# A transformer-like stack in one launch: the mixer's block sums move ahead of three steps of a gemm, and a copy on VectorE moves ahead of a subtraction

## The reference

```python
u = rmsnorm(h, norm_mix[l])
proj = u @ w_in[l]
u_ssm, q, k, v = jnp.split(proj, [D_SSM, D_SSM + D_ATTN, D_SSM + 2 * D_ATTN], axis=-1)
y_ssm = s5_branch(u_ssm, ...)              # x_t = Abar x_{t-1} + Bbar u_t, y_t = Re(C x_t) + D u_t
y_attn = stick_breaking_attention(q, k, v) # A[t,s] = beta[t,s] * prod_{s<j<t} (1 - beta[t,j])
```

## Time and profile before

| | |
|---|---|
| median of three runs | 1427.44 us (1426.12 to 1428.05) |
| the profiled execution | 1426.22 us |
| its span (first to last instruction) | 1424.4 us |
| TensorE busy | 1387.7 us, 97% of the span |
| VectorE busy | 962.6 us, 68% |
| ScalarE busy | 736.3 us, 52% |
| granted TensorE clock, mean | 0.995 |
| the four steps of the mixer | about 44 to 226 us of the span |

### The profile page before, as it was taken

One profiled execution on the slowest core, in us unless ns is written; L12 is line 12 of the kernel. 1 busy time (PEld: TensorE's weight loads), 2 busy tenths in 40 slices (PEclk: granted clock), 3 DMA queues, 4 the chain that ended last, 5 costly groups with the idle time before them and its releaser, 6 DMA issues.

```text
span 1424.4 us, 18408 instructions
## 1 busy us (share of the span) xinstructions
PE 1387.7 (97%) x6984; PEld 1163.5 (82%) x6984; DVE 962.6 (68%) x1343; ACT 736.3 (52%) x1038; POOL 70.8 (5%) x81
## 2 busy tenths in 40 slices
PE   7999999999999999999999999999999999999997
PEld 4888888788888888888877999878878888887876
DVE  7989984424654445444469777554879999998574
ACT  6777776222432223222246444333558888888452
POOL 2000000000200000000020000002100000000311
PEclk9999999999999999999999999999999999999998
DMA  6111102222222232322221211222221121211311
GB/s 222 43 60 60 60 27 92 89 95 107 94 89 89 99 109 89 103 86 106 89 89 60 89 59 59 104 89 89 89 89 60 61 86 59 85 63 44 119 60 59
DMA packets 19241, 118.22 MB, mean 83 GB/s; under 512 B 2400, under 2 KB 3680, under 8 KB 5616
## 3 DMA queue, kind: packets, MB, share of 16 engines
q1 hardware_dynamic: 18896, 116.38, 22.9%
q0 software_dynamic: 288, 1.05, 0.2%
HBM read 115.32 MB, written 2.10 MB: 82 GB/s over the span
## 4 chain that ended last, share of the span: by engine, by line
PE 75%; DVE 8%; ACT 3%; issue 2%; POOL 0%; DVEq 0%; POOLq 0%; ACTq 0%
PE ps L520 23%; PE ps L522 23%; PE ps L521 22%; PE ps L1015 1%; DVE wlo L1832 1%; PE ps L1048 1%; PE ps L1005 1%; PE ps L1046 1%; DVE st L2314 1%; PE ps L1007 1%; DVE stlo L2317 1%; ACT sthi L1193 1%; POOL pp L503 0%; ACT whi L1193 0%; PE ps L616 0%
## 5 line engine op out<-in xcount | busy, mean ns | idle before, releaser
L520 PE MATMUL ps<-uhi,whi 128*128 128x512 f32 x1100 | 436.3, 397 | 7.8 <-DVE ulo L2351 3.7
L522 PE MATMUL ps<-uhi,wlo 128*128 128x512 f32 x1100 | 429.7, 391 | 0.0
L521 PE MATMUL ps<-ulo,whi 128*128 128x512 f32 x1100 | 428.9, 390 | 0.0
L1832 DVE TENSOR_TENSOR wlo<-wraw,whi 128x2048 fp32r<-128x2048 f32 x104 | 241.0, 2320 | 98.7 <-ACT whi L1193 97.2
L1193 ACT ACTIVATE whi<-wraw 128x2048 fp32r<-128x2048 f32 x105 | 200.3, 1908 | 162.4 <-PE ps L522 160.5
L520 PEld LDWEIGHTS ps<-uhi,whi 128*128 128x128 f32 x1100 | 207.0, 188 | 55.5 <-issue 6.4
L522 PEld LDWEIGHTS ps<-uhi,wlo 128*128 128x128 f32 x1100 | 206.7, 188 | 44.6
L521 PEld LDWEIGHTS ps<-ulo,whi 128*128 128x128 f32 x1100 | 207.2, 188 | 40.0
L520 PE MATMUL ps<-hdhi,whi 128*128 128x512 f32 x256 | 99.6, 389 | 0.0
L521 PE MATMUL ps<-hdlo,whi 128*128 128x512 f32 x256 | 99.6, 389 | 0.0
L522 PE MATMUL ps<-hdhi,wlo 128*128 128x512 f32 x256 | 99.6, 389 | 0.0
(11 more groups left out here) (444 smaller groups left out, 2460.9 us busy)
## 6 DMA issues: line engine op xcount, KB each, us to landing
wraw<-wstream SPq DMA_DIRECT2D x105, 1024.0 KB, 4.8
h<-xT SPq DMA_DIRECT2D x4, 512.0 KB, 5.5
outT<-h SPq DMA_DIRECT2D x8, 256.0 KB, 2.9
s5b<-s5p_d SPq DMA_DIRECT2D x1, 1024.0 KB, 12.2
pe_in<-pT POOLq DMA_DIRECT2D x2, 512.0 KB, 3.8
cst_in<-cst_d SPq DMA_DIRECT2D x5, 64.0 KB, 10.1
reset<-cst_d SPq DMA_DIRECT2D x1, 256.0 KB, 11.2
ones<-cst_d SPq DMA_DIRECT2D x1, 64.0 KB, 2.5
```

The lines of the kernel that those rows point to most:

```text
L520: nc.tensor.matmul(out, lh, rh, start=start, stop=False, skip_group_check=True)
L521: nc.tensor.matmul(out, lh, rl_, start=False, stop=False, skip_group_check=True)
L522: mm = nc.tensor.matmul(out, ll, rh, start=False, stop=stop, skip_group_check=True)
L1832: V.tensor_tensor(wlo[:, slot, :], wraw[:, slot, :], whi[:, slot, :], ALU.subtract).then_inc(lo_done, 1)
```

## The change

On TensorE, the gemm of the next q is cut in two: five of its eight steps stay in their place, then the block sums and the triangle follow, and the other three steps come behind the triangle, ahead of the kernels. On VectorE, the copy that repeats the input maps leaves `turn_in` and becomes a function of its own, `repeat_maps`, called between `softplus(0)` and `fail_lo(0)`; since it overwrites Es, which the block sums read, it now carries the wait for them.

```diff
@@ -742,9 +742,10 @@
                 scores(0)
                 u_blocks(i)
                 pe.wait_ge(v_ready, i + 1)
-                gemm(n, 0, one(0), 256, uhi, ulo)
+                gemm(n, 0, one(0), 256, uhi, ulo, part=range(5))
                 block_sums()
                 log_weights(0)
+                gemm(n, 0, one(0), 256, uhi, ulo, part=range(5, DC))
                 kernels()
                 scores(1)
@@ -2063,16 +2064,20 @@
+                def repeat_maps():
+
+                    dve.wait_ge(f_done, 2 * i + 1)
+                    dve.wait_ge(in_gen, i + 1)
+                    V.tensor_copy(Es[:, :, :].rearrange("p r (q j c) -> p (r q) j c", q=QP, j=L),
+                                  ET[:, :, :, 0:1, :].rearrange("p r q j c -> p (r q) j c").to_broadcast([P, 2 * QP, L, 32])
+                                  ).then_inc(rep_ready, 1)
+
                 def turn_in():
                     f = ps[:, S0:S0 + 2, :].rearrange("p r (q n) -> p r q n", q=QP)
                     dve.wait_ge(f_done, 2 * i + 1)
                     dve.wait_ge(table_ready, i + 1)
                     own.do(V.tensor_tensor(rin[:, :, :, :], f, cos2, ALU.mult))
                     V.tensor_tensor(zst[:, :, :, :], f, sin2, ALU.mult).then_inc(f_used, 1)
-                    dve.wait_ge(in_gen, i + 1)
-                    V.tensor_copy(Es[:, :, :].rearrange("p r (q j c) -> p (r q) j c", q=QP, j=L),
-                                  ET[:, :, :, 0:1, :].rearrange("p r q j c -> p (r q) j c").to_broadcast([P, 2 * QP, L, 32])
-                                  ).then_inc(rep_ready, 1)
@@ -2119,6 +2124,7 @@
                 out_maps(i)
                 softplus(0)
+                repeat_maps()
                 fail_lo(0)
                 turn_in()
                 w_lo(0)
```

## The result

| | before | after |
|---|---|---|
| median | 1427.73 us (11 runs, 1426.12 to 1428.83) | 1430.77 us (11 runs, 1429.50 to 1432.80) |
| profiled execution | 1426.22 us | 1430.61 us |
| its span | 1424.4 us | 1428.8 us |
| first scores of step 0 to second scores of step 3 | 45.20 to 197.06: 151.86 us | 45.32 to 200.58: 155.26 us |

The ratio of after to before is 1.0024, 95% interval 1.0016 to 1.0032: the change makes the kernel slower, by 3.4 us with an interval of 2.3 to 4.6 (the two medians are 3.04 us apart). The forecast was 1.8 us, which I called no change; the median lies just inside the range given, 1427.3 to 1431.0.

What follows compares the result with a forecast made beforehand. The prediction took TensorE to bound the mixer, hardly waiting there. Step costs 0.49 + 0.41 + 0.41 + 0.49 = 1.80 us, put on the median of 1427.44, gave 1429.2 us, range 1427.3 to 1431.0.

Steps and rivals of the forecast that it cites:

- What bounds the mixer: In the mixer's four steps TensorE hardly waits, so each microsecond lost in a step's head reaches the program's end.
- The new wait for athi: Between block sums and triangle TensorE would newly wait 1.45 us in steps 1 to 3; step 0's wait becomes 2.46.
- The copy on VectorE: Between softplus and low half the copy into Es fits in idle time, 0.45 us ahead of 100.20, and costs nothing.
- The kernels' wait goes, and they take 1.70: Behind the three late gemm steps the kernels no longer wait (1.06 us before) and take 1.70 us.
- 0.49 per step, 0.41 where VectorE's chain has room: Second scores come 0.49 us later per step; steps 1 and 2 pass on 0.41, steps 0 and 3 all 0.49.
- The clock: Rival: step 0's 2.46 us wait makes TensorE's clock fall, costing 1.7 us more, 1430.9 us in all; 7 in 100.
- the two rivals at 1430.8 and 1430.9: VectorE's low half pushed back, 1430.8 us, 5 in 100; one clock fall in step 0, 1430.9 us, 7 in 100.
- The rival of the pushed low half: Late block sums delay VectorE's copy, so atlo slips 0.4 us and a step costs 0.9: 1430.8 us; 5 in 100.

Runs made afterwards that it cites:

- e4: The change in steps 1 to 3 alone, step 0 ordered as before: mixer 153.33 us (before 151.86), time ratio to before 1.0004.
- e3: The change plus eight matmuls with unread results in step 0's wait for athi: mixer 153.85 us (with the change 155.26), time ratio to before 1.0013.
- e1: The kernel before with TensorE's gemm cut 5 + 3 alone, VectorE's copy in its old place: mixer 155.30 us, time ratio to before 1.0026.
- e8: The change in step 0 alone, steps 1 to 3 ordered as before: mixer 153.80 us, time ratio to before 1.0013.
- e2: The kernel before with VectorE's copy into Es moved alone, the gemm whole: mixer 155.04 us, time ratio to before 1.0038.
- e5: The change with the gemm cut 6 + 2 instead of 5 + 3: mixer 153.17 us, time ratio to before 0.9999.
- e6: The kernel before with the gemm cut 7 + 1, the copy into Es in its old place: mixer 151.78 us, time ratio to before 1.0004.
- e9: The kernel before with the copy into Es made by GpSimd instead of VectorE: mixer 151.75 us (before 151.86), time ratio to before 0.9998.
- e10: As e9, and half of VectorE's scan moved ahead of the first weights' low part: mixer 149.52 us, time ratio to before 0.9992.
- e7: The kernel before with second scores ahead of the kernels on TensorE, ScalarE and VectorE reordered to match: mixer 154.65 us, time ratio to before 1.0026.

## Why the prediction was wrong, point by point

- **What bounds the mixer: right.** TensorE waits hardly anywhere, and what it loses in the head of a step stays lost. e4 and e3 show about 0.5 us per step arriving at the end of the stretch.
- **The new wait for athi: right in kind and size.** I computed 1.45 us in steps 1 to 3 from start to start, and got 102.29 - (99.17 + 1.70) = 1.42; in step 0 2.46, and got 2.45. The view of waits counts less (1.18 and 2.18, 5.8 in all where I had written 6.5 to 7), as it counts from the modelled end of the last matmul.
- **The copy on VectorE: right.** It fits into the idle time, 0.42 us ahead of athi where I had said 0.45; e1 shows that it also buys nothing.
- **The kernels' wait goes, and they take 1.70: right.** 109.09 - 107.39 = 1.70.
- **0.49 per step, 0.41 where VectorE's chain has room: right to 0.1.** Measured 0.54, 0.52 and 0.52 in steps 1 to 3, with 0.06 to 0.07 given back between steps. Without the clock the sum is 3.40 - 1.44 = 1.96 us, and 1.99 in e3, where 1.80 stood in the sum.
- **The clock: this is the step that failed.** The sum put the clock at nothing. I wrote the mechanism down with its place, one fall in step 0, and its price, "1.8 + 1.7 = 3.5, so 1430.9", but gave it 7 in 100. The fall came in all three profiles of this order in step 0 (after, e1, e8), and cost 1.44 us where 1.7 was written. My grounds were that a wait of 1.36 us in step 0 had left the clock at 1.00. A wait 1.8 times as long is outside of what such a row can vouch for. The trace of before has nearer rows, which the prediction did not read: TensorE waits 2.11 us for ulo until 936.33, and the granted clock stays at 1.00; it waits 2.43 us for rstd until 1416.45, and the granted clock is 0.57 from 1416 to 1422, though only one matmul runs there. One of two is no ground for 7 in 100. The rule cited from the Trainium skill, "TensorE: Matmul & The Clock Gate", section "Loop structure matters more than you think", pointed the right way; the trace agrees with it here, with 0.50 granted after a wait of 2.18 us, and does not in other places (last section).
- **The chances.** With the forecast's sum of 1.8 so near to the 2.85 us that bound no change, a term of 1.4 to 1.7 us decided between no change and slower. The case that carried it had to be settled before the other digits. That the median, 1430.77, lies inside the range says nothing for the forecast's own sum: the range reached up to the two rivals at 1430.8 and 1430.9.
- **The rival of the pushed low half** did not occur in the change; e2 shows it, with 0.86 us of wait for atlo in step 1.

## What to carry to other kernels

A wait that ends a chain on another engine is not shortened by giving the waiting engine its work in another order: before work is moved out of a place, ask what runs beneath it, here the 6.8 us from ScalarE's first function of the scores (93.39) to athi (100.17), and compare its length with the work that remains. Where a move leaves TensorE standing in one piece, look through the whole trace for waits of that length, read the granted clock behind each, and give a fall of the clock a chance to match; then check whether work already due can stand there (e5 and e6; e3 shows it with work that nobody needs). And a wait removed on TensorE pays only if the list that ends the loop gets shorter too: e6 and e9 cut the wait ahead of the kernels from 4.1 us to 2.4 and 1.5 and gained next to nothing, e10 took 0.57 us off each of steps 0 to 2 by filling VectorE's idle time.

## What the runs showed of the hardware that I had not expected

**Waits and the clock.** The length of a wait does not by itself decide whether the granted clock falls. The same waits stand in many of the twelve profiles, and the clock behind them differs. The table has every place behind 10 us and ahead of 1400 us where TensorE waited 1.5 us or more; a fall is a granted clock of 0.72 on the mean of the 6 us behind the wait, and without one it is 1.00. (Near 1420 us all twelve wait 2.43 us and have the clock fall or low already, but TensorE runs next to nothing behind that wait.)

| place | wait, us | profiles with it | with a fall |
|---|---|---|---|
| step 0 of the mixer, for athi | 2.17 to 2.18 | after, e1, e8 | all three |
| the same | 1.52 | e5 | that one |
| 753 to 759 us, ahead of a gemm | 2.24 to 2.25 | after, e1, e5, e6, e7, e9 | e5, e7, e9 |
| 933 to 942 us, for ulo | 2.10 to 2.11 | all twelve | e6 |
| 1296 to 1306 us, for ulo | 1.57 to 1.60 | all twelve | e3, e5, e7, e10 |

Two of those that left the clock alone, in before and in after:

```profile
936.33 0.47 PE L520 MATMUL ps<-uhi,whi 128*128 128x512 f32 x1 [2.11 <-DVE ulo L2351]
```

```profile
936.00:942.00 6.00, 5.67 (x25) 4.72 (x26) 5.54 (x9) 5.86 (x9) 0.00 (x0) 1.00 0.00 0
```

```profile
757.39 0.47 PE L520 MATMUL ps<-uhi,whi 128*128 128x512 f32 x1 [2.25 <-issue]
```

```profile
757.00:763.00 6.00, 5.61 (x24) 4.37 (x25) 5.82 (x10) 2.75 (x5) 0.00 (x0) 1.00 0.37 153
```

So behind the same instruction, in code that no edit touches, the clock falls in one profile and not in another. That the wait is the cause in step 0 rests on the mixer's own runs: a fall in each of the three profiles with 2.2 us and in the one with 1.52, and none in the mixer of the other eight, whose longest wait there is 1.36 us. What decides behind a given wait was not tried, and three profiles give no rate.

A fall costs 1.1 to 1.6 us, by place. From the wait near 1300 us to the wait for rstd near 1420 the eight profiles without a fall take 117.13 to 117.21 us and the four with one 118.26 to 118.27, so 1.1 us; in e6 the stretch from 936.80 to 1062.64 is 1.55 us longer than its like in before (125.84 against 124.29); in the mixer it was 1.44. A wait's price is its length, and with some chance that much more.

**Falls that move the whole time.** Between the feed-forward part and the attention with gates (740 to 782 us) the clock falls in every profile, but at different times and for different lengths. Before, and then after:

```profile
740.00:770.00 30.00, 27.91 (x110) 18.15 (x108) 26.46 (x47) 13.64 (x19) 4.81 (x4) 0.94 0.15 57
770.00:782.00 12.00, 12.00 (x68) 10.35 (x67) 10.85 (x14) 11.74 (x12) 0.00 (x0) 0.86 0.26 89
```

```profile
740.00:770.00 30.00, 26.86 (x117) 18.68 (x115) 26.36 (x46) 13.65 (x19) 5.63 (x4) 1.00 0.21 71
770.00:782.00 12.00, 12.00 (x36) 7.59 (x36) 9.91 (x15) 9.77 (x10) 0.00 (x0) 0.72 0.16 53
```

This is where the spans' difference of 4.4 us has most of what the mixer's 3.40 leaves over: 0.12 us were lost ahead of the mixer and 0.8 between 737 and 805 us, in code that the change does not touch. Of the other profiles e2, e4 and e8 lost 1.7 us against before in this stretch, e3 and e10 less than 0.1. The wait ahead of the gemm there also differs, 1.38 us in some profiles and 2.25 in others. What sets the moment of the fall there was not tried.

**VectorE and GpSimd in each other's way.** In step 0 of e9 and of e10, GpSimd's copy and VectorE's low half start within 0.01 us of each other. In e9 first VectorE, then GpSimd; and then the same two in e10:

```profile
54.89 2.37 DVE L2116 TENSOR_TENSOR atlo<-att,athi 128x1280 fp32r<-128x1280 f32 x1 [1.34 <-ACT athi L1199]
```

```profile
54.88 1.04 POOL L500 COPY Es<-ET 128x1024 f32<-128x1024 f32 x1 [34.65 <-PE ps L670]
```

```profile
54.82 1.49 DVE L2116 TENSOR_TENSOR atlo<-att,athi 128x1280 fp32r<-128x1280 f32 x1 [1.34 <-ACT athi L1199]
```

```profile
54.83 2.38 POOL L500 COPY Es<-ET 128x1024 f32<-128x1024 f32 x1 [34.27 <-PE ps L670]
```

The one that starts 0.01 us later takes 2.4 us, about both durations in a row: 1.04 + 1.49 = 2.53. In e9 that is VectorE, and TensorE then waits 0.8 us for atlo; this is the 0.52 us that step 0 of e9 lost. In step 1 of e9 GpSimd's copy starts at 101.55, with VectorE's low half running from 100.62 for 1.49 us, and takes 1.47 instead of 1.04: about the 0.56 us that the low half had left, and its own time. The Trainium skill, "SBUF — State Buffer", section "SBUF: two separate sides", says that VectorE, when both its inputs lie in SBUF, and a GpSimd instruction that reads SBUF share a port pair, and that the one that starts first holds it for the whole of its instruction. The low half reads att and athi from there, and the two pairs of rows agree with it.
